# Transposing turns by halves of the channels in eight banks, and weight splits ahead of the norm behind the experts

## What is computed

```python
for layer in range(DEPTH):                       # DEPTH = 2
    h = _rmsnorm(x, norm1_g[layer])
    proj = h @ w_in[layer]
    ...
    x = x + mix @ w_o[layer]
    h2 = _rmsnorm(x, norm2_g[layer])
    x = x + jnp.square(jax.nn.relu(h2 @ w_up[layer])) @ w_down[layer]
```

```python
x = layer_norm(DN_ALPHA * x + m, ln1_g[i], ln1_b[i])
f = hier_moe(x, ...)                             # 32 experts, two per token
x = layer_norm(DN_ALPHA * x + f, ln2_g[i], ln2_b[i])
```

## Time and profile before

| | |
|---|---|
| median of three runs | 3486.24 us |
| the profiled execution | 3483.18 us |
| its span | 3481.9 us |
| mean granted clock of PE, as a share of full speed | 0.967 |
| busy PE / DVE / ACT | 3237.2 / 2227.0 / 1804.5 us |

### The profile page before, as it was taken

The page is one execution under the profiler, slowest core; times in us unless marked ns, Lnnn a source line. Parts: engine busy times, 40 slices in busy tenths (PEclk is TensorE's granted clock), DMA queues, the critical chain, the costliest instruction groups (busy, mean ns, idle before and its releaser), DMA issues.

```text
span 3481.9 us, 41985 instructions
## 1 busy us (share of the span) xinstructions
PE 3237.2 (93%) x16554; PEld 2687.4 (77%) x16555; DVE 2227.0 (64%) x3412; ACT 1804.5 (52%) x2691; POOL 378.1 (11%) x333
## 2 busy tenths in 40 slices
PE   8899999999989999999988999999789889999995
PEld 6788777877888787878676777888577868888884
DVE  5755442435855443434666888899743669998886
ACT  3333342323333342324463788888533638888884
POOL 1111000000111000000140111111100111111110
PEclk9999999999999999999998999999899989999998
DMA  3210222221120222222104899988723248899995
GB/s 140 74 58 1 73 97 81 90 97 50 59 74 1 73 97 73 97 91 91 50 1 167 347 358 357 354 353 360 269 73 109 76 192 334 356 361 355 365 355 183
DMA packets 135161, 590.90 MB, mean 170 GB/s; under 512 B 29744, under 2 KB 35632, under 8 KB 110256
## 3 DMA queue, kind: packets, MB, share of 16 engines
q1 hardware_dynamic: 115664, 569.85, 42.3%
q0 software_dynamic: 19296, 18.30, 2.2%
HBM read 594.34 MB, written 44.04 MB: 183 GB/s over the span
## 4 chain that ended last, share of the span: by engine, by line
PE 37%; DMA 5%; DVE 5%; ACT 3%; issue 1%; SPq 0%; POOL 0%; DVEq 0%; ACTq 0%; POOLq 0%
PE ps L190 33%; DMA mem<-in_w_up 4%; PE ps L3406 1%; DMA mem<-in_w_gate 1%; DVE r L3526 1%; ACT r L3471 1%; PE ps L3447 1%; PE ps L2509 0%; DVE mem L2625 0%; ACT mem L3496 0%; DVE r L2937 0%; DVE r L2759 0%; ACT mem L2568 0%; DVE mem L2954 0%; ACT r L2904 0%
## 5 line engine op out<-in xcount | busy, mean ns | idle before, releaser
L190 PE MATMUL ps<-r,r 128*128 128x512 f32 (+2 forms) x10920 | 2573.9, 394 | 64.7 <-DVE r L2139 23.2
L190 PEld LDWEIGHTS ps<-r,r 128*128 128x128 f32 (+1 forms) x10920 | 2025.7, 190 | 532.9 <-issue 63.2
L3526 DVE TENSOR_TENSOR r<-mem,r 128x1024 fp32r<-128x1024 f32 x768 | 903.0, 1222 | 131.1 <-ACT r L3471 123.4
L3471 ACT ACTIVATE r<-mem 128x1024 fp32r<-128x1024 f32 x768 | 788.5, 1061 | 220.8 <-PE ps L190 146.0
L693 ACT ACTIVATE r<-mem 128x512 fp32r<-128x512 f32 (+3 forms) x518 | 340.2, 664 | 896.4 <-PE ps L190 889.9
L728 DVE TENSOR_TENSOR r<-mem,r 128x512 fp32r<-128x512 f32 (+1 forms) x256 | 175.0, 689 | 421.3 <-ACT r L693 419.9
L730 DVE SCALAR_TENSOR_TENSOR r<-mem,r 128x512 fp32r<-128x512 f32 (+3 forms) x262 | 183.8, 717 | 277.5 <-ACT r L693 275.8
L3384 POOL DMA_INDIRECT xa<-mem,memu x64 | 102.5, 1601 | 961.7 <-ACT mem L3496 946.7
L3324 POOL DMA_INDIRECT mem<-xd,memu x64 | 98.6, 1540 | 60.0 <-PE ps L3406 35.7
L1700 PE MATMUL ps<-mem 128*128 128x65 f32 x800 | 99.5, 282 | 0.0
L1700 PEld LDWEIGHTS ps<-mem 128*128 128x128 f32 x800 | 96.4, 199 | 0.0
(11 more groups left out here) (406 smaller groups left out, 2814.4 us busy)
## 6 DMA issues: line engine op xcount, KB each, us to landing
mem<-in_w_up SPq DMA_DIRECT2D x80, 2048.0 KB, 18.3
mem<-in_w_down SPq DMA_DIRECT2D x80, 2048.0 KB, 8.0
mem<-in_w_gate SPq DMA_DIRECT2D x64, 2048.0 KB, 13.4
mem<-in_w_in SPq DMA_DIRECT2D x10, 2048.0 KB, 7.8
mem<-in_odd_w_qkv SPq DMA_DIRECT2D x6, 2048.0 KB, 7.9
mem<-in_w_o SPq DMA_DIRECT2D x4, 2048.0 KB, 10.7
mem<-in_rel SPq DMA_DIRECT2D x16, 512.0 KB, 3.3
mem<-in_even_w_in SPq DMA_DIRECT2D x3, 2048.0 KB, 8.1
```

The lines of the kernel that those rows point to most:

```text
L190: r = e.matmul(out, a, b, start=start and i == 0, stop=stop and i == n - 1, skip_group_check=skip)
L3471: act.e.activation(wh, w, ACT.Copy).then_inc(*self.S["ex_wh"](self.l, e, i))
L3526: dve.e.tensor_tensor(wl, w, wh.bitcast(F32), SUB).then_inc(*self.S["ex_wl"](self.l, e, i))
```

## The change

1. A turn that is a stage of its own, and the column turn of `tail_0`, works in the order 0, 2, 4, 6, 1, 3, 5, 7: the lower half of the channels of all tiles first. Each unit has a bank of its own (even units banks 0 to 3, odd ones 4 to 7), and no unit waits for a bank. In `tail_0` PE keeps the order 0 to 7.
2. The product behind such a turn doesn't wait for the turn's end. Its piece kk waits for the four units of its half (`ready` and `half`). The field that named the mixer's output stage is renamed from `source` to `mix`.
3. In `tail_0`, the three copies and three subtractions of the next product's weights are issued ahead of the norm. ACT copies units 0 and 1 between its third and fourth root, 2 and 3 behind the fourth, and then 4, 6, 5, 7.

```diff
@@ class Turn
+        self.split = prev is not None
+        self.order = (0, 2, 4, 6, 1, 3, 5, 7) if self.split else range(8)
     def ps(self, u):
-        return self.K.bank[self.first + u % 4][:, :].rearrange("p (k n) -> p k n", k=4)
+        bank = u // 2 + u % 2 * 4 if self.split else self.first + u % 4
+        return self.K.bank[bank][:, :].rearrange("p (k n) -> p k n", k=4)
     def pe_unit(self, pe, u):
-        if u >= 4:
+        if u >= 4 and not self.split:
             pe.wait_ge("nx_lo", self.name, u - 4)
...
-        for u in range(8):
+        for u in self.order:
...
+    def half(self, pe, kk):
+        for t in range(4):
+            pe.wait_ge("nx_lo", self.name, 2 * t + kk // 4)
@@ class Dense
+        self.source = prev if isinstance(prev, Turn) else None
     def enter(self, pe):
-        pe.wait_end(self.entered)
+        if self.source is None:
+            pe.wait_end(self.entered)
     def ready(self, pe, job, kk):
-        pass
+        if self.source:
+            self.source.half(pe, kk)
@@ class Mixer, pe
-        pe.wait_end(self.entered)
+        self.enter(pe)
         for i, (job, kk) in enumerate(self.plan):
             pe.wait_ge("dn_lo", self.p0 + i)
+            self.ready(pe, job, kk)
@@ class ColumnTurn
+        if into:
+            self.split, self.order = True, (0, 2, 4, 6, 1, 3, 5, 7)
@@ class Tail, act
         act.wait_end(self.prev)
+        if self.turn:
+            self.follow.begin_act(act, 3)
         for t in range(4):
             var = self.mv[:, t, 1:2]
             act.wait_ge("ln_v", sid, t, "var")
             act.e.activation(var, var, ACT.Sqrt).then_inc(*S["ln_a"](sid, t, "root"))
+            if self.turn and t >= 2:
+                self.turn.act_unit(act, 2 * t - 4)
+                self.turn.act_unit(act, 2 * t - 3)
         if self.turn:
-            self.follow.begin_act(act, 3)
-            for u in range(8):
+            for u in (4, 6, 5, 7):
                 self.turn.act_unit(act, u)
@@ class Tail, dve
         dve.wait_ge("d_ln", self.gains.names)
+        if self.turn:
+            self.follow.begin_dve(dve, 3)
...
         if self.turn:
-            self.follow.begin_dve(dve, 3)
-            for u in range(8):
+            for u in self.turn.order:
                 self.turn.dve_unit(dve, u)
@@ stages
             tail.follow = add(Dense, "odd_proj", list(Odd.jobs(K, lo)))
+            tail.follow.source = turn
```

More of the change, by code:

```diff
@@ L2996, in __init__ @@
     def __init__(self, K, name, prev, l, chunk, lo, source=None):
-        self.l, self.source = l, source
+        self.l, self.mix = l, source
         self.gains = Gains(K, l, "ln1", K.o1 + 6144)
@@ L3059, in enter @@
     def enter(self, pe):
-        if self.source is None:
-            pe.wait_end(self.entered)
+        if self.mix is None:
+            super().enter(pe)
     def ready(self, pe, job, kk):
-        if self.source is not None:
-            pe.wait_ge("em_lo", self.source.name, "x", kk)
+        if self.mix is None:
+            super().ready(pe, job, kk)
+        else:
+            pe.wait_ge("em_lo", self.mix.name, "x", kk)
     def normed(self, t):
```

## The result

The changed kernel takes 3490.36 us (median) against 3482.39 us of the kernel before, measured beside each other. The ratio is 1.0020 with an interval of 1.0012 to 1.0029. The forecast was 3480, a little faster. One of the changed kernel's twelve executions (5229.46 us, at a mean granted clock of 0.573) and one of the kernel before in the series of e5 to e7 (6382.48 us) were in a slow state and are left out of the ratios; without the first the changed kernel's median is 3490.20 us. The profiled execution of the changed kernel took 3491.19 us.

A forecast was written before the change was run, and what follows sets the result against it. PE, busy 93% of the span, was taken as the bound. Terms -6.0 (tail), -0.3 (start), +1.7 (clock falls) and -1.4 (odd_proj's clock) sum to -6.0 us; against the median 3480.2, taken as 3480, range 3475 to 3485.

The forecast's parts named there:

- Parts 1 and 2: In tail_0, splits ahead of the norm, eight banks and order by halves start the product 6.0 us earlier.
- Part 3: Half entry gives 0 us in mix_0, mix_1, mix2_1, as splits queue behind the whole turn; norm1_0 gains 0.3 us.
- Part 4: Longer PE gaps at mix_0, mix_1, mix2_1 may lower the clock: 0 to 8.7 us lost, taken as +1.7.
- The 1.4 us gain of odd_proj's clock: Behind tail_0 the product follows transposes after less idling, so its clock is higher; -1.4 us, bounds 1.7 gain to 0.6 loss.
- (b): All three grown gaps are caught, 2.9 us loss each, 8.7 against 6.3 won; 3488.6 us, chance 0.04.
- (a): Clock is kind: no turn falls and odd_proj's product is warm; -8.0 us, so 3478, chance 0.27.
- (c): Half entry works at every turn, four halves at four places, 9.8 us more; 3470, chance 0.04.
- (d): In tail_0 first weights come late or ACT's copies delay the last root, halving the 6.0 us gain; 3483, chance 0.08.

The follow-up runs named there:

- e5: Kernel before, but its four stand-alone turns use eight banks and PE waits for no bank; 3496.21 us against 3483.14, ratio 1.0044.
- e7: Kernel before with only the splits of odd_proj's first three pieces moved ahead of the norm in tail_0; 3480.84 us in a single execution.
- e1: Changed kernel with only tail_0 and odd_x changed, the four stand-alone turns as before; 3476.26 us against 3482.41 of the kernel before.
- e6: Changed kernel with splits ahead of and between turn units in mix_0, mix_1, mix2_1; 3470.45 us against 3483.14 of the kernel before.
- e3: Changed kernel with PE's wait for the unit four places earlier put back in stand-alone turns; 3478.10 us against 3482.41 of the kernel before.
- e2: Changed kernel with only stand-alone turns and their half entry changed, tail_0 and odd_x as before; 3493.48 us against 3482.41 of the kernel before.
- e4: Changed kernel plus 16 unneeded PE transposes before the products behind the four stand-alone turns; 3478.95 us against 3482.41 of the kernel before.

## Why the prediction was wrong

**Parts 1 and 2 (the tail): right.** 5.7 us against 6.0. The 0.3 us are DVE's: from its first half at 2547.16 to the product at 2551.33 are 4.17 us, in e1 too (2527.49 to 2531.66), where 2530.86 to 2534.7, 3.84 us, were worked out. It waited for nobody in between; the eight halves ran without a pause in 8.43 us, 1.05 each instead of the 0.91 of the earlier trace rows. Why a half takes longer in this order is open.

**Part 3 (the other turns): right in its mechanism.** The product's start did not move in mix_0, mix_1 and mix2_1 (0.1 us), and at the start it came at 18.58 instead of 19.08, 0.5 us for the 0.3 forecast. That 0.5 can't be told from chance: in e7, where this stage is as before, the product began at 18.36. e6 showed the queue order to be the reason why the half entry gave nothing.

**Part 4 (the clock): the step that failed.** The mechanism was named and even bounded at 8.7 us, but it went into the sum with +1.7, one fall more. The runs showed 12.3 us at the median in its place, the difference of e3 and the changed kernel. In the profiled executions three things were too small:
- The number of falls. Of the nine gaps of 2.0 to 2.6 us I took six falls as a sign that three grown gaps would be hardly worse off. But the three places in question had all been spared. Two of the three were caught in the changed kernel, all three in e2. A gap at mix_0 or mix_1 of 2.3 or 2.4 us kept its clock in the profiles of before, e1 and e3; the gap of 3.3 to 3.4 lost it at both places in the changed kernel and e2, and at mix_0 in e5. At mix2_1 length alone did not decide: 2.56 us kept it before, 2.55 and 2.39 lost it in e1 and e3, 3.45 kept it in the changed kernel and lost it in e2.
- The price of one. It was taken as 1.7 us from the earlier trace rows. Here it is 2.8, since the fall comes inside the gap and the low level then lasts over 5.7 us of the product. The 2.9 us were worked out and kept for the rival only. The row behind 1.7 us, 2541.47 to 2544.88, is of a fall that came 0.74 us after the product had begun. The fall inside the 2.39 us gap at 1068.94 was followed by the low clock over all of the 8.60 us of work read there, so the trace of before showed that a fall can cost well over 1.7 us:

```profile
1071.40:1080.00 8.60, 8.60 (x37) 8.31 (x38) 0.77 (x3) 3.12 (x6) 0.00 (x0) 0.50 0.00 0
```

- What follows a fall. In the changed kernel the feed-forward parts behind out_0 and out_1 start at the low clock too, although their own gap is about as before. No term of the prediction had this. Each of the two stretches up to and with the next big gap grows by 1.4 us, as these windows of before and after show:

```profile
429.64:524.40 94.76, 88.98 (x384) 72.08 (x385) 43.67 (x68) 43.49 (x73) 0.00 (x0) 0.98 0.25 89
...
1218.33:1313.95 95.62, 89.83 (x384) 72.01 (x385) 43.67 (x68) 43.37 (x73) 0.00 (x0) 0.99 0.25 89
```

```profile
434.25:530.44 96.19, 90.40 (x385) 73.13 (x385) 43.59 (x68) 43.40 (x73) 0.00 (x0) 0.98 0.25 88
1229.53:1326.56 97.03, 91.24 (x384) 73.07 (x385) 43.56 (x68) 43.34 (x73) 0.00 (x0) 0.97 0.25 87
```

That gives 2.8 + 2.7 + 1.4 + 1.4 = 8.3 us in this execution, and mix2_1, spared here but caught in e2, adds 2.9 us where it is. Three more stretches of the profiled execution are longer, though nothing was edited in them and the matmul work is the same: the two mixers of the first block by 2.5 us each (352.34 to 354.79 and 635.68 to 638.20) and the one that begins at 1598.20 before and 1612.11 after by 1.4 (104.09 to 105.48). There the product began at the low clock (0.64 over 3.89 us) behind a gap of 1.73 us, where it was 1.62 before. With the 5.7, 1.5 and 0.5 us won at the tail, in odd_proj and at the start, this comes to 7.0 of the 8.0 us between the two profiled executions. How much of the three stretches is tied to the edit stays open. The second mixer takes 637.9 us in e4 as well, which has no fall at mix_0 or mix_1 and a good time, so that one is no mark of the damage. How the 12.3 us of the medians divide is therefore not shown beyond these 8.3 us, or 11.2 where mix2_1 is caught.

The 1.4 us gain of odd_proj's clock, forecast with -1.4, came in the profiled execution: its 576 matmuls took 133.4 us instead of the 134.9 of the earlier trace rows. In e1, e3, e4 and e6, whose tail is the same, they took 134.7 to 134.8, and the product began at the low clock. So the term was met by luck in one of five profiles.

The level was helped by luck as well. It was set from a median of three, 3486.24 us, and twelve executions of the kernel before gave 3482.39. The forecast change was -6.2 us and the measured one +8.0, a miss of 14.2 us, while 3480 and 3490.36 are only 10.4 apart.

**The rivals.** It went nearest to (b), which had a chance of 0.04: grown gaps are caught, at 2.8 us each, and the clock outweighs the tail. But (b) decides from 6.3 us of loss on, and the two gaps caught in the profiled execution make only 5.5; the falls before the feed-forward parts, which (b) did not have, carry it over. (a) is refuted by the windows at out_0, (c) by the earlier trace rows and the timeline after, until e6 makes it true in another way, and (d) by the tail's interval. mix2_1's gap of 3.45 us was caught in e2 and missed in the changed kernel, while at mix_0 a gap of 3.3 or 3.4 us was caught in each of the three profiles that have it. The rule of the Trainium skill ("TensorE: Matmul & The Clock Gate", section "What's actually happening") that the activity monitor runs freely agrees with the first, and with the two of e2's twelve executions that lost nothing, and not visibly with the second.

**What the trace of before could have told.** Two kinds of gap were compared by length alone, while the question was how much room each of three places had left. With all gaps of 4.1 us and over caught, 3.3 us deserved at least even odds at three places. At the 2.9 us of rival (b) each that is 4.4 us, the sum would have been -3.3 us, and the forecast no change with both signs open. The 8 us slower that was measured would still have been missed.

## What to carry to other kernels

A wait that spreads an engine's work over the time in which it would be idle anyway may be worth keeping: taking PE's bank waits away made its work no earlier where it counted and its idle stretch 0.9 to 1.0 us longer, and that cost 11 to 13 us (e2, e3, e5). Before letting a product in early, look at what stands ahead of its first operands in each in-order queue; with the first split ahead of the turn and the next two between its halves, at three places, the same edit was worth 12.7 us against the kernel before. When an edit lengthens a gap of PE at full clock, price the half-speed work behind it in the forecast itself, not beside it.

## What the runs showed of the hardware

- At mix_0 and mix_1 the clock's answer to idling was steep: with 2.3 to 2.4 us of gap the product behind took 51.1 to 51.2 us, with 3.3 to 3.4 us 53.8 to 53.9, and no product came out between. One gap of 2.75 us (mix_1 in e5) kept the clock, at 51.26 us. At mix2_1 it was not so: gaps of 2.39 and 2.55 us were caught (e3, e1) and one of 3.45 was not (changed kernel).
- Sixteen unneeded transposes, 1.9 us of PE's time, were as good as the wait: e4 and e3 are 0.9 us apart.
- After a fall at mix_0 or mix_1 the next one came before the feed-forward part, at a gap of 1.7 us, in all five cases: twice in the changed kernel, twice in e2, and at mix_0 in e5. In e4, in e6 and at mix_1 in e5, where the gap is the same 1.7 us but no fall came ahead of it, none came. That a fall brings on another one some 50 us later fits this, but was not tried by itself.
- The gap of PE before the feed-forward parts is 1.72 instead of 1.62 us in kernels without the bank waits, though the code there is untouched. The cause is open. Before the feed-forward parts of e4 and e6 it cost nothing but itself, but two other gaps that grew in this way from 1.62 us were caught: that before 1612.11 in the changed kernel (1.73 us) and that before 817.72 in e5 (1.72 us).
